# A two-layer decoder trunk: x comes in transposed by DMA at the mixer's entry, in place of turns on TensorE

## The reference, cut to what matters

```
def rms_norm(x, w, eps=1e-6):
    y = x * lax.rsqrt(jnp.mean(x * x, axis=-1, keepdims=True) + eps)
    return y * w

u = rms_norm(x, norm_pre_mix[0])
zxbcdt = u @ in_proj            # 2048 x 10304
# z | xs | B | C | dt: gate, conv input, state inputs, time steps (last 64 columns)
dt = softplus(dt_raw + dt_bias)
```

## Time and profile before

| | |
|---|---|
| median of 3 runs | 2521.73 us (2521.62 to 2521.81) |
| the profiled execution's own time | 2523.18 us |
| its span | 2521.2 us |
| PE busy | 2506.2 us, 99% |
| DVE busy | 1822.3 us, 72% |
| ACT busy | 1247.9 us, 49% |
| POOL busy | 155.6 us, 6% |
| DMA | 474.10 MB, mean 188 GB/s |
| chain that ended last | PE 98%, DVE 1%, ACT 1% |
| a split on ACT (L664), mean | 1059 ns |
| its low half on DVE (L993), mean | 1242 ns |

### The profile page before, as it was taken

One profiled execution on the slowest core, in us unless ns is written; L12 is line 12 of the kernel. 1 busy time (PEld: TensorE's weight loads), 2 busy tenths in 40 slices (PEclk: granted clock), 3 DMA queues, 4 the chain that ended last, 5 costly groups with the idle time before them and its releaser, 6 DMA issues.

```text
span 2521.2 us, 42149 instructions
## 1 busy us (share of the span) xinstructions
PE 2506.2 (99%) x15444; PEld 2238.8 (89%) x15444; DVE 1822.3 (72%) x2572; ACT 1247.9 (49%) x1631; POOL 155.6 (6%) x271
## 2 busy tenths in 40 slices
PE   8999999999999999999999999999999999999999
PEld 8999999999898888888888998998898888888887
DVE  6977877787876675766667876778866667576667
ACT  7555555554654444444444754455644444444444
POOL 2222112211100000000000000000000000000000
PEclk9999999999999999999999999999999999999999
DMA  7666556656566566666656555555566656666664
GB/s 216 212 199 199 175 184 192 206 166 196 172 190 193 183 197 189 191 191 190 192 183 198 194 176 176 179 173 168 184 189 188 192 183 198 190 191 192 190 192 151
DMA packets 267240, 474.10 MB, mean 188 GB/s; under 512 B 16673, under 2 KB 50066, under 8 KB 265618
## 3 DMA queue, kind: packets, MB, share of 16 engines
q1 hardware_dynamic: 264194, 457.53, 59.2%
q0 software_dynamic: 2624, 15.00, 1.7%
q10 hardware_dynamic: 336, 0.41, 0.0%
HBM read 470.70 MB, written 2.19 MB: 188 GB/s over the span
## 4 chain that ended last, share of the span: by engine, by line
PE 98%; DVE 1%; ACT 1%; DMA 0%; issue 0%; SPq 0%; ACTq 0%; DVEq 0%
PE ps L1615 23%; PE ps L1616 23%; PE ps L1617 23%; PE ps L1644 16%; PE ps L1646 9%; PE ps L1873 1%; PE ps L1751 0%; PE ps L1971 0%; DMA h<-x 0%; PE ps L1878 0%; PE ps L1810 0%; PE ps L1779 0%; PE ps L2001 0%; PE ps L1729 0%; PE ps L1735 0%
## 5 line engine op out<-in xcount | busy, mean ns | idle before, releaser
L993 DVE TENSOR_TENSOR whl<-raw,whl 128x1024 fp32r<-128x1024 f32 x856 | 1062.5, 1242 | 592.1 <-ACT whl L664 579.5
L664 ACT ACTIVATE whl<-raw 128x1024 fp32r<-128x1024 f32 x856 | 906.7, 1059 | 1086.8 <-PE ps L1617 735.9
L1644 PE MATMUL ps<-xhl,whl 128*128 128x512 f32 x1792 | 623.0, 391 | 0.0
L1646 PE MATMUL ps<-xhl,whl 128*128 128x256 f32 x1792 | 505.4, 282 | 0.0
L1615 PE MATMUL ps<-whl,bhl 128*128 128x512 f32 x1284 | 500.8, 390 | 0.0
L1616 PE MATMUL ps<-whl,bhl 128*128 128x512 f32 x1284 | 499.5, 389 | 0.0
L1617 PE MATMUL ps<-whl,bhl 128*128 128x512 f32 x1284 | 499.5, 389 | 0.0
L1615 PE MATMUL ps<-xhl,whl 128*128 128x256 f32 x1748 | 493.9, 283 | 0.0
L1616 PE MATMUL ps<-xhl,whl 128*128 128x256 f32 x1748 | 488.5, 279 | 0.0
L1617 PE MATMUL ps<-xhl,whl 128*128 128x256 f32 x1748 | 487.9, 279 | 0.0
L1644 PEld LDWEIGHTS ps<-xhl,whl 128*128 128x128 f32 x1792 | 336.4, 188 | 70.9
(11 more groups left out here) (268 smaller groups left out, 2084.6 us busy)
## 6 DMA issues: line engine op xcount, KB each, us to landing
raw<-mlp_w SPq DMA_DIRECT2D x512, 512.0 KB, 4.2
raw<-a_in_proj SPq DMA_DIRECT2D x161, 512.0 KB, 4.5
raw<-a_out_proj SPq DMA_DIRECT2D x64, 512.0 KB, 4.0
raw<-b_w_q SPq DMA_DIRECT2D x32, 512.0 KB, 4.0
raw<-w_k SPq DMA_DIRECT2D x32, 512.0 KB, 4.0
raw<-w_v SPq DMA_DIRECT2D x32, 512.0 KB, 3.6
raw<-b_out_proj SPq DMA_DIRECT2D x32, 512.0 KB, 3.7
cumb<-cum_scratch POOLq DMA_DIRECT2D x8, 1024.0 KB, 7.7
```

Of the source, the lines that this page charges most:

```text
L664: sc.activation(slot_of(s, lo)[0], raw_of(s), ACT.Copy).then_inc(hi_ready, 1)
L993: ve.tensor_tensor(out=low, in0=raw_of(s), in1=hi.bitcast(F32), op=ALU.subtract).then_inc(lo_ready, 1)
L1644: te.matmul(ps[:, f, :].rearrange("p (q n) -> p q n", q=2), wh[:, j, c], xboth[:, :, k, :], start=k == 0, stop=False, skip_group_check=True)
L1646: last = te.matmul(ps[:, f, 0:S], wl[:, j, c], xhi[:, k, :], start=False, stop=k == KT - 1, skip_group_check=True)
```

## The change

The host hands over a second array, `x_t`, x transposed (2048 by 256). SP loads it in five pieces into `xt`, which is the room of `y` seen with features on the partitions. The pieces stand between the loads of slabs: two tiles behind slab 0, two behind slab 1, four behind slab 2, four behind slab 4 and four behind slab 5 (the dt slab). The nine loads of `par_rows` move from behind slab 3 to behind slab 5 and the last piece.

The factor of a token now has to stand along the free axis: DVE puts the factors on a diagonal (`diagonal`), PE multiplies a matrix of ones by it (`spread_rs(0)`), ACT copies the result to `rs_row`. The function and its line were there for later norms. Then `xt` is multiplied by `rs_row` in place: pair 0 by DVE, pairs 1 to 7 by POOL, a pair at a time, behind POOL's eight DMA starts and ahead of its table. ACT's `x_tile` and DVE's correction read `xt` in SBUF where they read PSUM. The 32 turns of `y` on PE and the scaling of `y` by ACT and DVE are gone. On ACT and DVE the order is now slab by slab: split k, pair k, for all eight pairs. The identity turns ahead of the first slab go from 4 to 8.

```diff
-X_PIECES = ((0, 256), (256, 512), (512, 1024), (1024, 1536), (1536, 2048))
+X_TILES = ((0, 2), (2, 4), (4, 8), (8, 12), (12, 16))
 X_PIECE = (0, 1, 2, 2, 3, 3, 4, 4)
+X_BEHIND = {0: 0, 1: 1, 2: 2, 4: 3, 5: 4}
-AWAKE, FIRST_AWAKE = 24, (10, 13, 4)
+AWAKE, FIRST_AWAKE = 24, (10, 13, 8)
@@ SP
                 mix_load(mix.slab(k), unit, i, 0)
-                if k == LEAD - 1:
+                if k in X_BEHIND:
+                    lo, hi = X_TILES[X_BEHIND[k]]
+                    sp.dma_start(xt[:, lo:hi, :], w["x_t"][lo * P:hi * P, :].rearrange("(k p) s -> p k s", p=P))\
+                        .then_inc(xt_in[X_BEHIND[k]], 16)
+                if k == LEAD + 1:
                     sp.wait_ge(rows_cleared, 2)
@@ POOL
+            pool.wait_ge(rs_row_ready, 1)
+            for i in range(1, KT // 2):
+                pool.wait_ge(xt_in[X_PIECE[i]], 16)
+                pair = xt[:, 2 * i:2 * i + 2, :]
+                g_.tensor_tensor(out=pair, in0=pair, in1=rs_row[:, :].unsqueeze(1).to_broadcast([P, 2, S]), op=ALU.mult)\
+                    .then_inc(x_scaled, 1)
@@ ACT
             split(mix.slab(0))
-            x_halves(0, (0, 1), 0)
-            split(mix.slab(1))
-            scale_x(2)
-            split(mix.slab(2))
-            x_halves(0, (2, 3), 0)
-            split(mix.slab(3))
-            scale_x(3)
-            scale_x(4)
+            spread_rs(0)
+            x_halves(0, (0,), 0)
+            for k in range(1, LEAD):
+                split(mix.slab(k))
+                x_halves(0, (k,), 0)
@@ ACT and DVE, the steps behind the first four slabs
-                if unit == "xs" and i < 2:
-                    x_halves(0, ((4,), (5, 6, 7))[i], 0)
+                if unit == "xs" and i < KT // 2 - LEAD:
+                    x_halves(0, (LEAD + i,), 0)
@@ DVE
-            for n in range(2):
-                lo, hi = X_PIECES[n]
-                for t in range(MT):
-                    ve.tensor_scalar(y[:, t, lo:hi], h[:, t, lo:hi], rsh[:, t:t + 1], None, ALU.mult).then_inc(x_scaled[n], 1)
+            diagonal(rsh, rms_ready)
+            dve.wait_ge(xt_in[0], 16)
+            dve.wait_ge(rs_row_ready, 1)
+            ve.tensor_tensor(out=xt[:, 0:2, :], in0=xt[:, 0:2, :], in1=rs_row[:, :].unsqueeze(1).to_broadcast([P, 2, S]),
+                             op=ALU.mult).then_inc(x_scaled_first, 1)
@@ PE
             for k, (unit, i) in enumerate(MIX_FIRST):
-                for n in FIRST_TURNS.get(k, ()):
-                    transpose_scaled_x(n)
                 if k == 0:
+                    spread_rs(0)
                     keep_awake(FIRST_AWAKE[2], 0)
                 if k < 4:
-                    high_first(mix.slab(k), i, (2, 3) if k == 1 else ())
+                    high_first(mix.slab(k), i)
```

More of the change, by code:

```diff
@@ L69 @@
               ((5, 7), (6, 6), (2, 2), (7, 7), (5, 5), (6, 6), (2, 2), (7, 7)), MLP_TURNS)
-SPREAD_BANK = (None, 6, 2, 6)
+SPREAD_BANK = (6, 6, 2, 6)
 AWAKE_BANK = 2
@@ L384, in build @@
         x_in = [sem(f"x_in{n}") for n in range(PIECES)]
-        x_scaled = [sem(f"x_scaled{n}") for n in range(len(X_PIECES))]
+        xt_in = [sem(f"xt_in{n}") for n in range(len(X_TILES))]
+        x_scaled_first, x_scaled = sem("x_scaled_first"), sem("x_scaled")
         heads_in, rel_in, lam_in = sem("heads_in"), sem("rel_in"), sem("lam_in")
@@ L679, in x_tile @@
                 k = 2 * i + j
-                return sc.activation(dst[:, k, :], ps[:, TURN_BANKS[r][i][j], j * S:(j + 1) * S], ACT.Copy,
-                                     scale=par[:, col + k:col + k + 1])
+                src = xt[:, k, :] if r == 0 else ps[:, TURN_BANKS[r][i][j], j * S:(j + 1) * S]
+                return sc.activation(dst[:, k, :], src, ACT.Copy, scale=par[:, col + k:col + k + 1])
             def x_half(r, i, dst, col, done):
-                act.wait_ge(xt_done, KT // 2 * r + i + 1)
+                if r > 0:
+                    act.wait_ge(xt_done, KT // 2 * (r - 1) + i + 1)
+                elif i > 0:
+                    act.wait_ge(x_scaled, i)
+                else:
+                    act.wait_ge(x_scaled_first, 1)
                 x_tile(r, i, 0, dst, col)
@@ L1271, in _ @@
             inverse_by_root(rsh, sum_h, ssh_and_eps, 1)
-            for n in range(2):
-                lo, hi = X_PIECES[n]
-                for t in range(MT):
-                    ve.tensor_scalar(y[:, t, lo:hi], h[:, t, lo:hi], rsh[:, t:t + 1], None, ALU.mult).then_inc(x_scaled[n], 1)
-            dve.wait_ge(par_ready, 1)
[L1277 to L1282, removed]
+            diagonal(rsh, rms_ready)
[3 more added lines that the diff above has]
+                             op=ALU.mult).then_inc(x_scaled_first, 1)
+            dve.wait_ge(par_ready, 1)
+            for k in range(LEAD):
+                split(mix.slab(k))
+                x_halves(0, (k,), 0)
             def lambdas():
@@ L1706, in output, with high_first @@
                 token_major(s, i % 2, 2, banks[nt], block)
[L1708 to L1714, removed]
-                        k = 2 * i + j
-                        last = te.transpose(ps[:, TURN_BANKS[0][i][j], j * S + t * P:j * S + (t + 1) * P], y[:, t, k * P:(k + 1) * P],
-                                            ident[:, :])
-                last.then_inc(xt_done, 1)
-            def high_first(s, i, turns=()):
+            def high_first(s, i):
                 pe.wait_ge(hi_ready, s.n + 1)
@@ L1730, in high_first @@
                               skip_group_check=True)
-                for n in turns:
-                    transpose_scaled_x(n)
                 pe.wait_ge(lo_ready, s.n + 1)
@@ L2105 @@
                                    kind="ExternalInput").ap()
+    arrays["x_t"] = np.ascontiguousarray(inputs["x"][0].T)
+    aps["x_t"] = nc.dram_tensor("x_t", (D, S), F32, kind="ExternalInput").ap()
     out = nc.dram_tensor("out", (1, S, D), F32, kind="ExternalOutput").ap()
```

19 lines of the change are left out of this document (8 added, 11 removed).

## The result

| | before | changed |
|---|---|---|
| median of 6 runs | 2521.77 us (2521.62 to 2522.13) | 2531.86 us (2530.05 to 2533.73) |
| the profiled execution's own time | 2523.18 us | 2531.37 us |
| span | 2521.2 us | 2529.4 us |
| dt slab's matmuls, first | 33.22 | 39.02 |
| DVE's copy of their result (`cumt`) | 37.22 | 44.68 |

The ratio is 1.0039, with a 95% interval of 1.0029 to 1.0049: slower by 10.1 us. The profiled executions differ by 8.2. In that of before x landed late: the factor's last step stands at 13.75, and at 12.63 in that of the changed kernel, 1.1 us sooner. With that added the profiles give 9.3.

What follows compares the result with a forecast made beforehand. PE bounds the kernel, so only the dt matmuls' start counts; DVE's lengthened row moves it from 33.22 to 40.7. Turns -2.6, first matmul +0.9 and PE's waits make +7.5 on 2521.73: 2529.2 us, range 2525 to 2533.5.

Steps and rivals of the forecast that it cites:

- rival 1: PE's clock falls while it stands 3.6 us ahead of the dt matmuls: +3.7 us, 2532.9 us; chance 0.20.
- DVE's row: DVE's work before the dt matmuls: 17.4 us from 15.75, plus 7 POOL products at 1.0 each; step by step, 40.6.
- the first matmul: PE's first real matmul, behind diagonals, spread, copy, product and ACT's tiles: at 17.4, 0.9 us later than before.
- PE's waits: PE waits 0.5 and 2.0 us inside slab 0 and 3.6 us ahead of the dt matmuls.
- The moment: The change is worth the shift of the dt slab's first matmul, 33.22 before; nothing behind the entry swallows or adds.
- Corrections collide: DVE's corrections, now reading `xt` in SBUF, contend with POOL's products like the subtractions: 1.0 us each time.
- Rival 4: `rs_row` after 16.2 lets POOL's product precede DVE's pair 0: first matmul 1.2 us later, 2530.4; counted in the forecast's 0.37.
- rival 2: Only some or no instructions collide: 2526.3 or 2525.2, with the clock's fall 2530.0 or 2528.9; chance 0.23 with fall, 0.15 without.
- The sum: Whole kernel +7.5 us: turns -2.6, first matmul +0.9, the rest PE's waits in slabs 0 to 4 and before dt.
- The loads: SP's nine small loads take 5.1 us; the seventh slab lands at 33.4, its split hidden behind DVE by 1.9 us.
- Rival 3: POOL delays nothing and the nine loads take under 3.1 us: dt matmuls at 33.3, 2521.8 us; chance 0.05.
- The turns' gain: Removed turns and the later first matmul alone would start the dt matmuls at 31.4, 1.8 us earlier than before.

Runs made afterwards that it cites:

- run 1: The changed kernel with POOL's seven products left out, pairs 1 to 7 staying unscaled: 2532.08 us.
- run 9: The changed kernel with POOL's first product made to wait for DVE's product of pair 0: 2531.65 us.
- run 5: The changed kernel with 26 identity turns on PE between slab 4 and the dt slab's wait: 2530.07 us.
- run 3: The changed kernel with pairs 5, 6 and 7 split and corrected right behind the dt slab's split, as in the kernel before: 2527.05 us.
- run 4: The changed kernel with the seven products on DVE in place of POOL, each behind a slab's low half: 2532.78 us.
- run 2: The changed kernel with POOL's seven products left out and the nine small loads back behind slab 3: 2530.57 us.
- run 7: The kernel before with pairs 5 to 7 split and corrected one slab at a time, behind slabs 6, 7 and 8: 2524.90 us.
- run 6: The changed kernel with only the nine small loads moved back behind slab 3: 2532.43 us.
- run 11: Changed kernel: products on DVE, slab 0's low half first, pairs 5 to 7 behind the dt split, small loads late, `x_t` pieces recut, 18 identity turns: 2524.54 us.
- run 8: Changed kernel: small loads behind slab 3, pairs 5 to 7 behind the dt split, products on DVE, slab 0's low half before the first: 2525.81 us.

## Why the prediction was right, and where its steps were off

Slower was right (0.77), and 2531.86 lies in the range of 2525.0 to 2533.5, between the forecast of 2529.2 and rival 1's 2532.9: it is the forecast's mechanism, DVE's row ahead of the dt slab, with about half of rival 1's loss by the clock on top. That the number is so near is in part luck, since the first matmul was 1.6 too late, PE's waits lay elsewhere, and the 0.7 us further down had no term.

- **The moment.** That one moment decides, the dt slab, holds: see the sums just above, and PE's busy time from 100 to 2500 us.
- **DVE's row: right, with errors that cancel.** It began at 14.62 (15.75 forecast), of which x came 1.1 sooner. The seven collisions cost 1.52 (2.21 less 0.69), 2.06, 2.17 and 1.92 for the three doubled pairs: 7.7 us, 7.0 forecast. The bare work was 16.7 and not 17.4. So its end was 38.97 and not 40.6, and with the earlier start taken out the forecast was 0.5 too long, about what its step by step count had added in waits for transfers.
- **Corrections collide: right.** No row of before could show it. Two of them with two products take 2.79 to 3.04 us, and with none 0.87. The Trainium skill's rule in "SBUF — State Buffer", "Who interferes with whom" (two SBUF inputs on DVE against a GpSimd read) gave this, and the trace agrees; run 1 shows that it is the products.
- **PE's waits lay elsewhere.** I had 0.5 and 2.0 us inside slab 0 and none ahead of slab 4. There was none inside slab 0, where POOL's second product waited for `x_t` until 18.90 and DVE's corrections of pair 0 went undisturbed, and 1.89 ahead of slab 4, behind the doubled corrections of pair 4 (30.02). Of the seven collisions six hit corrections, and none the low halves of slabs 2 and 3. DVE's sum is the same either way.
- **Rival 4's effect came without its condition.** It needed `rs_row` later than POOL's last DMA start, and `rs_row` was there at 14.51, that DMA start ended at 14.98. DVE's product began when forecast (14.62 with x 1.1 sooner, 15.75 forecast), but POOL's got its turn first: 2.21 us, and the first matmul at 17.91, which is 1.6 later than 17.4 less 1.1. Most of it is DVE's time again, as the prediction said; run 9 shows that undoing it brings nothing at the end.
- **The clock fell: rival 1.** From the first dt matmul to the last are 5.27 us (44.29 less 39.02), before 3.61 (36.83 less 33.22): 1.7 us, where rival 1 had all 32 at the lower clock and 3.7. PE's wait was 3.08 us. With the matmuls at the full clock in run 5 the same stretch took 3.71. The length of the wait alone doesn't tell (last section). The fall had 0.43 in all (0.20, and 0.23 within rival 2), and the forecast was made without it: that is the step which failed, and most of the 2.7 us. It was looked for only ahead of the dt slab; the fall in slabs 0 and 1 wasn't thought of, and run 3 shows a fall in slab 4 that does cost something once DVE's row is shorter.
- **The sum again.** Start of the dt matmuls 39.02 less 33.22 is 5.8, plus 1.1 for x is 6.9 (7.5 forecast); 1.7 for the clock; 0.7 open: 9.3, the profiles' difference. The medians say 10.1; the changed kernel's runs spread over 3.7 us, before's over 0.5, and its profiled run is 0.5 below its median.
- **The loads: hidden, but by 1.0 us and not 1.9, and with a price behind it that I hadn't.** "Hidden behind DVE" was true of the changed kernel and no longer where DVE's time was cut. Runs 1, 4 and 9 removed DVE time and met the slab's landing at 32.7, 35.2 and 34.1; run 2 met it at 32.3 even with the small loads out of the way. I had taken an `x_t` piece's issue as free; it took 3.12 us, and up to 8.08 in the other runs. The Trainium skill, "Perfetto Trace Analysis", "Per-instruction lifecycle", says that such a row ends once all descriptors of the transfer have been generated, and that a DMA engine may begin on them before that, particularly if more are generated than the descriptor buffer holds. The rows agree in direction: an issue of 0.47 us at 18.40, where the DMA engines were busy 0.55 of the time, and of 3 to 8 us where they were busy 0.89 and more. That a full buffer is the cause is not shown by any run here.
- **Rival 2 priced run 1 wrongly.** With no collision I had the dt matmuls at 36.7 and 2525.2 us, or 2528.9 with the clock's fall; they began at 38.04 in run 1, and it took 2532.08. The step that failed is the landing at 30.3: it was 32.7, because the nine loads began at 23.81 and not at 20.8, behind a piece of `x_t` whose issue I had as free. With the small loads away, in run 2, it was 32.3.
- **Rival 3** had no run near it: the nine loads took 5.1 us as forecast (23.58 to 28.68), here behind a queue already late.
- **The turns' gain** of 1.8 us never showed, for the same reason: up to 39 us PE's row was no longer the longest.

The order of the last pairs, two subtractions more or 2.5 us in the forecast, was worth 4.8 us in run 3 and 3.1 in the kernel before (run 7). By the profiles run 3 gained 4.2: 1.9 at the dt slab's start, 1.7 by the clock behind it, and the 0.7 of the longer steps. The rest of the 10.1 isn't additive: runs 1, 4, 6 and 9 each took away one bound and gained nothing.

## What to carry to other kernels

When a row that feeds PE is as long as PE's own, count every instruction ahead of the last tile PE needs, and keep work that PE needs only later behind it: that order was worth 4.8 and 3.1 us here, about as much as all 32 turns (3.5). An elementwise product given to POOL isn't free if DVE's work beside it reads two operands from SBUF; price it as DVE's time. Before believing in a gain from one bound, work out where the next one stands (here 1.0 us behind), and count a load's issue on its queue in a stretch where the DMA engines are full. And look at the granted clock of every stretch behind a wait of PE, not only at the one that you expect.

## What the runs showed of the hardware

- DVE's product has its start in the record at 14.62 and POOL's at 15.00, and still POOL's ran at its bare 1.27 us and DVE's took 2.21: the earlier start in the record didn't hold the turn. Run 9's wait reverses it. What decides it stays open.
- The issue of a 512 KB piece of `x_t`, in rows of 1 KB, took SP 0.47 us at 18.40 in the changed kernel, and 3.12 for the last one; in the other runs the last one took 3.36 to 6.77, and in run 11, though half as large, 8.08. The load of a 512 KB slab, rows of 2 KB, took 0.37 at 20.00 just ahead of it.
- The 32 small copies of POOL's table took 9.88 us in the changed kernel, 14.24 in run 8, and 5.91 before; nothing that PE wanted stood behind them. Why they differ isn't shown.
- PE's granted clock fell to 0.50 (distances of 0.21 us in place of 0.117) behind some of its waits. Behind those of 5.09 to 7.80 us (runs 1, 2, 4 and 6) it was low each time. Among the shorter ones it was low behind 1.45 (run 8), 1.93 (run 11), 1.95 (run 3), 2.58 (run 5), 2.60 (run 6, ahead of the first slab), 2.73 (run 9) and 2.95 and 3.08 (changed kernel), at once or up to a microsecond later, and stayed up behind 1.82 (run 7), 1.89 (changed kernel) and 2.96 (run 5). So the length of the wait alone doesn't decide; what does stays open. A fall at the changed kernel's dt slab cost 1.7 us.
